# Opening of a mixer and expert-gather kernel reordered by tile, with half of a weight loaded a second time

## The reference

```python
p = (h @ w_in)                        # h: rmsnorm(x), scaled and shifted
rq, rk, rv, rg, gq, gk, gv, gg, lr_f, lr_b = split(p)
ret = head_rmsnorm(o_rf + flip(o_rb)) * silu(rg)     # retention, 4 heads x 128
gla = head_rmsnorm(o_gf + flip(o_gb)) * silu(gg)     # gated linear attention, 4 heads x 128
x = x + g1 * (concat([ret, gla]) @ w_out)
h = modulate(rmsnorm(x, norm2_w), sh2, sc2)
# peer_ffn, for each block of 128 tokens:
q = h @ w_q                                          # 8 heads x 2 halves x 128
s1, s2 = q[..., 0] @ k1.T, q[..., 1] @ k2.T          # 128 keys each
idx = top16 of (top16(s1) + top16(s2))               # one of 128 * 128 experts
act = gelu(einsum("thkd,td->thk", down[idx], h))
x = x + g2 * einsum("thkd->td", (softmax(top) * act) * up[idx])
```

## Time and profile before

| | |
|---|---|
| median of 3 runs | 3169.85 us (3169.84 to 3169.93) |
| span of the profiled execution | 3165.3 us |
| PE busy | 2588.5 us, 82% |
| DVE busy | 2022.9 us, 64% |
| ACT busy | 1229.5 us, 39% |
| POOL busy | 1074.3 us, 34% |
| software DMA queue (the gathers) | 1073.81 MB, 82.1% of 16 engines' span |

### The profile page before, as it was taken

The page is one execution under the profiler, slowest core; times in us unless marked ns, Lnnn a source line. Parts: engine busy times, 40 slices in busy tenths (PEclk is TensorE's granted clock), DMA queues, the critical chain, the costliest instruction groups (busy, mean ns, idle before and its releaser), DMA issues.

```text
span 3165.3 us, 35978 instructions
## 1 busy us (share of the span) xinstructions
PE 2588.5 (82%) x12092; PEld 1064.0 (34%) x12092; DVE 2022.9 (64%) x5008; ACT 1229.5 (39%) x3892; POOL 1074.3 (34%) x1041
## 2 busy tenths in 40 slices
PE   7999998878777877778988878888777877978777
PEld 3555653323222323223333344333223332322111
DVE  4533457777777777665555757667777776765544
ACT  3122335443443444334323533444344543443323
POOL 0000014433433444333433334343443443343331
PEclk9999999899999989999999999999999999999999
DMA  9411359999999999999999999999999999999995
GB/s 353 155 54 53 125 204 405 421 421 418 415 420 421 419 408 414 418 417 411 418 415 417 416 411 393 416 419 421 420 418 417 416 419 416 405 420 422 418 421 243
DMA packets 198780, 1179.94 MB, mean 373 GB/s; under 512 B 20994, under 2 KB 21700, under 8 KB 67268
## 3 DMA queue, kind: packets, MB, share of 16 engines
q0 software_dynamic: 147456, 1073.81, 82.1%
q1 hardware_dynamic: 51140, 103.84, 8.9%
HBM read 1175.48 MB, written 2.10 MB: 372 GB/s over the span
## 4 chain that ended last, share of the span: by engine, by line
DMA 47%; PE 14%; ACT 5%; DVE 4%; issue 3%; POOL 3%; DVEq 0%; POOLq 0%
DMA ring<-in_expert_rows,idx_v 18%; DMA ring<-in_peer_rows,idx_v 11%; DMA scr<-in_expert_rows,idx_v 9%; DMA scr<-in_peer_rows,idx_v 8%; PE banks L1166 8%; PE banks L814 6%; DVE ring L2299 2%; POOL ring L788 1%; DVE scr L2299 1%; DMA scr<-in_w_in 1%; POOL scr L788 1%; ACT ring L1688 1%; ACT L1682 1%; ACT scr L1682 1%; ACT L1644 1%
## 5 line engine op out<-in xcount | busy, mean ns | idle before, releaser
L1166 PE MATMUL banks<-ring 128*32 128x512 f32 x2016 | 809.5, 621 | 251.7 <-ACT ring L1688 241.4
L1166 PE MATMUL banks<-scr,ring 128*32 128x512 f32 x2080 | 819.8, 613 | 215.5 <-ACT ring L1688 214.8
L1682 ACT ACTIVATE scr<-scr 128x1 f32<-128x1 f32 x1024 | 206.9, 202 | 1511.9 <-DVE scr L2299 1510.4
L2299 DVE CUSTOM_DVE_ANT_0 scr<-scr,ring 128x1024 f32<-128x1024 f32 x390 | 478.0, 1226 | 305.9 <-DMA scr<-in_peer_rows,idx_v 157.4
L2299 DVE CUSTOM_DVE_ANT_0 ring<-ring 128x1024 f32<-128x1024 f32 x378 | 463.1, 1225 | 302.0 <-DMA ring<-in_expert_rows,idx_v 166.7
L788 POOL DMA_INDIRECT scr<-in_peer_rows,idx_v x264 | 272.7, 1033 | 475.9 <-PE banks L1166 355.7
L814 PE MATMUL banks<-hT,scr 128*128 128x128 f32 (+3 forms) x2576 | 367.7, 303 | 66.4 <-DVE ring L2281 47.3
L1166 PEld LDWEIGHTS banks<-ring 128*32 128x32 f32 x2016 | 162.8, 111 | 770.2 <-ACT ring L1688 486.8
L788 POOL DMA_INDIRECT ring<-in_expert_rows,idx_v x256 | 271.1, 1059 | 422.1 <-PE banks L1166 389.3
L1166 PEld LDWEIGHTS banks<-scr,ring 128*32 128x32 f32 x2080 | 165.9, 111 | 737.3 <-ACT ring L1688 458.4
L788 POOL DMA_INDIRECT ring<-in_peer_rows,idx_v x248 | 263.1, 1061 | 409.4 <-PE banks L1166 371.0
(11 more groups left out here) (255 smaller groups left out, 2247.4 us busy)
## 6 DMA issues: line engine op xcount, KB each, us to landing
scr<-in_w_in SPq DMA_DIRECT2D x8, 2048.0 KB, 28.4
scr<-in_w_mod SPq DMA_DIRECT2D x7, 2048.0 KB, 12.8
ring<-in_w_in SPq DMA_DIRECT2D x7, 2048.0 KB, 12.8
scr<-in_w_q SPq DMA_DIRECT2D x6, 2048.0 KB, 27.8
ring<-in_w_mod SPq DMA_DIRECT2D x5, 2048.0 KB, 13.2
scr<-in_peer_w_q SPq DMA_DIRECT2D x4, 2048.0 KB, 12.3
scr<-in_peer_rows,idx_v POOLq DMA_INDIRECT x264
ring<-in_w_out SPq DMA_DIRECT2D x2, 2048.0 KB, 7.8
```

Source lines behind the costliest of these rows:

```text
L1166: last = nc.tensor.matmul(psum[2 + c][32 * g:32 * g + 32, :], spread[:, i % 8, :], rows[slot_of(i)][:, D + c * CW:D + (c + 1) * CW], start ...
L1682: nc.scalar.activation(gelu[:, h, k:k + 1], dots[:, h, k:k + 1], ACT.Gelu if i < N_ROWS else ACT.Gelu_apprx_tanh).then_inc(gelu_done, 1)
L2299: V.tensor_tensor_reduce(u, u, xq[g], 1.0, 0.0, ALU.mult, ALU.add, dots[:, n % 2, k:k + 1]).then_inc(dotted, 1)
```

## The change

Seven edits belong together.

1. The gate gg is made between the steps of the GLA part, and rg after it; `gla_gate` takes the place of `ret_gate`.
2. After the GLA outputs only tile 0 is gated with rg (8 k-products), turned (8 transposes) and multiplied by w_out. The rg products of tiles 1 to 3 stand in pieces behind, between and after the scores of head 0 and its index (`ret_gate_part`), the turning of these tiles after the gate of head 0 is moved (`turn_heads`). The silu of rg is written in place in its PSUM bank.
3. w_out for tile 1 is made in the opening and by pair 9. The second halves of tiles 2 and 3 come at pairs 26 to 34, their first halves at pairs 70 to 76.
4. So the first half of w_out is loaded a second time (`w_out_again`), into slots 0 and 1, when the last row before row 80 in them is summed.
5. Rows 0 to 79 have the slots 4 to 7, 0 and 1; rows 80 to 175 the slots 4 to 7, 2 and 3; eight slots are in use from row 176. Before it was from row 38.
6. Additions, means, squares, roots and normed outputs of tiles 1 to 3 move to later pairs and rows with them.
7. The order of the chunk loads follows the new order of use.

```diff
 SLOTS = 8
-OPENING = 38
+HALF_LEFT = 80
+ALL_LEFT = 176
...
-          (("w_mod", CW * 11), 3), (("w_in", W_GQK), 0), (("w_in", W_RG), 2), (("w_in", W_GV), 1), (("w_out", 0), 0),
-          (("w_in", W_GG), 1), (("w_out", CW), 2)]
+          (("w_mod", CW * 11), 3), (("w_in", W_GQK), 0), (("w_out", CW), 2), (("w_in", W_GV), 1), (("w_in", W_GG), 0),
+          (("w_in", W_RG), 1), (("w_out", 0), 0), (("w_out_again", 0), 0)]
...
-    if i < 4:
+    if i < 2:
         return 4 + i
-    if i < OPENING:
-        return (4, 5, 6, 7, 0, 1)[(i - 4) % 6]
-    return (2, 3, 0, 1, 4, 5, 6, 7)[(i - OPENING) % SLOTS]
+    if i < HALF_LEFT:
+        return (6, 7, 4, 5, 0, 1)[(i - 2) % 6]
+    if i < ALL_LEFT:
+        return (6, 7, 4, 5, 2, 3)[(i - HALF_LEFT) % 6]
+    return (6, 7, 4, 5, 2, 3, 0, 1)[(i - ALL_LEFT) % SLOTS]
...
+            sp.wait_ge(summed, max(i for i in range(HALF_LEFT) if slot_of(i) < 2) + 1)
+            load_chunk("w_out_again", 0)
...
-                elif slot < 4:
-                    full(pool, "wo", TT - 1, slot // 2)
+                elif slot in (6, 7):
+                    full(pool, "yT", TT - 1, 1)
+                elif slot in (0, 1):
+                    full(pool, "wo", 1, 0)
+                elif slot in (2, 3):
+                    full(pool, "wo", TT - 1, 1)
+                if i >= ALL_LEFT and slot in (0, 1) and previous(i) < HALF_LEFT:
+                    full(pool, "wo", TT - 1, 0)
...
+            def turn_heads(t):
+
+                pe.wait_ge(y_done, 1 + t)
+                empty(pe, "rg", t)
+                for half, src in ((0, o_ret), (1, o_gla)):
+                    o = begin("yT", t, half)
+                    for h in range(HEADS):
+                        last = nc.tensor.transpose(o[:, h * P:(h + 1) * P], src[:, t, h * P:(h + 1) * P], ident)
+                    last.then_inc(bank_ready, 1)
+
+            ret_gate_part(0, 0, KT)
+            turn_heads(0)
...
                 project("wo", 0, w)
-                o = opened("wo", 1, 0)
-                for k in range(KT // 2):
-                    mm(o[:, :], yT[:, k, P:2 * P], w[0][:, k, :], k, KT)
+                ret_gate_part(1, 0, 4)
                 tile_rows("n1", 0)
+                ret_gate_part(1, 4, 6)
                 all_empty(pe, "nt", "n1", 0, 1)
                 scores_q(0)
                 scores_s(0)
-                project("wo", 2, w, (0,))
+                ret_gate_part(1, 6, KT)
+                ret_gate_part(2, 0, KT)
                 quad_rows(0, 0, 0)
+                quad_rows(0, 1, 2)
+                ret_gate_part(3, 0, 2)
                 move_idx(0)
-                quad_rows(0, 1, 2)
-                pe.wait_ge(idx_packed, 1)
+                ret_gate_part(3, 2, KT)
                 move_gate(0)
...
+                for t in (1, 2, 3):
+                    turn_heads(t)
                 pe.wait_ge(xq_set, 2)
                 quad_rows(0, 2, 2)
                 quad_rows(0, 3, 0)
+                empty(pe, "rg", 3)
                 scores_q(1)
                 scores_s(1)
-                add_batch(0)
-                project("wo", 3, w, (0,))
-                add_pair(2)
+                empty(pe, "yT", 1, 0)
+                empty(pe, "yT", 1, 1)
+                add_row(0, True)
+                add_row(1)
+                project("wo", 1, w, (0,))
+                add_pair(1)
                 move_idx(1)
                 move_gate(1)
                 scores_q(2)
                 scores_s(2)
-                add_pair(3)
-                project_part("wo", 1, w, 0)
+                add_batch(1)
                 add_batch(2)
                 scores_q(3)
                 add_pair(6)
-                project_part("wo", 1, w, 1)
+                project_part("wo", 1, w, 0)
                 add_pair(7)
...
+                      8: lambda: project_part("wo", 1, w, 1),
+                      70: lambda: first_half_again(0), 72: lambda: first_half_again(1),
+                      74: lambda: project_part("wo", 3, w, 0, 0), 76: lambda: project_part("wo", 3, w, 1, 0),
```

More of the change, by code:

```diff
@@ L340, in plan_jobs @@
             jobs.add(("go", c, odd), "A")
-    for t in range(TT):
-        jobs.add(("gg", t), "A")
-    for k in range(KT):
-        jobs.add(("yT", k), alternate(k))
+    jobs.add(("rg", 0), "D")
+    for half in range(2):
+        jobs.add(("yT", 0, half), "AD"[half])
     for n in range(2):
@@ L347, in plan_jobs @@
     tile("n1", 0, (0, 1))
+    for t, bank in ((1, 6), (2, 7), (3, 5)):
+        jobs.add(("rg", t), "D", bank)
+    for t in (1, 2, 3):
+        for half in range(2):
+            jobs.add(("yT", t, half), "AD"[half], 6 + half)
+    for n in range(2):
+        jobs.add(("wo", 1, n), "D", 6 + n)
+    tile("n1", 1, (6, 7), "AA")
     for t, n, bank in LAST_HALVES:
         jobs.add(("wo", t, n), "D", bank)
-    for t in (1, 2, 3):
+    for t in (2, 3):
         tile("n1", t, (6, 7), "AA")
@@ L636, in _ @@
         def _(sp):
-            wide = {"w_mod": a["w_mod"][0], "w_in": a["w_in"][0], "w_out": a["w_out"][0]}
+            wide = {"w_mod": a["w_mod"][0], "w_in": a["w_in"][0], "w_out": a["w_out"][0],
+                    "w_out_again": a["w_out"][0]}
             def load_chunk(name, c0):
                 n = chunk_number(name, c0)
-                if chunk_before(n) is not None:
+                if name == "w_out_again":
+                    full(sp, "wo", 1, 0)
+                elif chunk_before(n) is not None:
                     chunk_read(sp, chunk_before(n))
@@ L1081, in _, with ret_gate_part @@
                     from_scores(c, h, BWD).then_inc(bank_ready, 1)
-            w = use_chunk("w_in", W_GG)
-            to_rows([("gg", t) for t in range(TT)], hT, w, TT)
-            for k in range(KT):
-                o = begin("yT", k)
-                pe.wait_ge(y_done, 1 if k < HEADS else 1 + TT)
-                src = o_ret if k < HEADS else o_gla
-                for t in range(TT):
-                    last = nc.tensor.transpose(o[:, t * P:(t + 1) * P], src[:, t, (k % HEADS) * P:(k % HEADS + 1) * P], ident)
-                last.then_inc(bank_ready, 1)
+            w_rg = use_chunk("w_in", W_RG)
+            def ret_gate_part(t, first, last):
+                o = psum[jobs.bank[jobs.number("rg", t)]]
+                if first == 0:
+                    opened("rg", t)
+                if last == KT:
+                    begin("rg", t)
+                for k in range(first, last):
+                    ins = mm(o[:, :], hT[:, k, t * P:(t + 1) * P], w_rg[:, k, :], k, KT)
+                if last == KT:
+                    ins.then_inc(bank_ready, 1)
+            def turn_heads(t):
[8 more added lines that the diff above has]
+            turn_heads(0)
             def project(name, t, w, halves=(0, 1)):
@@ L1187, in next_quads @@
             def next_quads(it, g):
-                if g == 0:
+                if g == 0 and it == 1:
+                    empty(pe, "wo", 2, 1)
+                    empty(pe, "wo", 3, 1)
+                elif g == 0:
                     name, t = ("n1", 3) if it < TT else (("gf", 0) if it == TT else ("gf", 3))
@@ L1438, in _ @@
                       472: lambda: products(2), 489: lambda: products(TT - 1)}
-            for t, first in ((2, 8), (3, 13)):
+            for t, first in ((2, 26), (3, 32)):
                 beside[first] = lambda t=t: project_part("wo", t, w, 0)
@@ L1632, in _, with ret_silu, heads_out @@
             nc.scalar.activation(hstat[:, 2, TT * HEADS:], hstat[:, 1, TT * HEADS:], ACT.Sqrt).then_inc(head_root, 1)
[L1633 to L1640 removed]
+            def ret_silu(t):
+                o = full(act, "rg", t)
+                nc.scalar.activation(o[:, :], o[:, :], ACT.Silu).then_inc(rg_silu, 1)
+            def heads_out(t):
+                copy_out(yT[:, 0:HEADS, t * P:(t + 1) * P], "yT", t, 0).then_inc(emptied["A"], 1)
+            ret_silu(0)
+            heads_out(0)
             def softmax_exp(n):
@@ L2167, in _ @@
             head_roots(1)
-            for t in range(TT):
-                head_scale(TT + t)
-                dve.wait_ge(y_step, TT + t + 1)
-                empty(dve, "gg", t)
-                V.tensor_tensor(o_gla[:, t, :], o_gla[:, t, :], gate_tmp[:, t % 2, :], ALU.mult).then_inc(y_done, 1)
-            for k in range(1, KT, 2):
-                o = full(dve, "yT", k)
-                V.tensor_copy(yT[:, k, :], o[:, :]).then_inc(emptied["D"], 1)
+            dve.wait_ge(gla_gated, 1)
+            dve.wait_ge(y_step, TT)
+            gate_gla(0)
+            gate_ret(0)
+            heads_out(0)
+            for t in (1, 2, 3):
+                gate_gla(t)
             empty(dve, "g1", 1)
@@ L2527, in _ @@
                       959: lambda: tile_mean("fin", 2), 963: lambda: final(2)}
-            for t in (1, 2, 3):
-                beside[13 + 8 * t] = lambda t=t: tile_mean("n1", t)
-                beside[17 + 8 * t] = lambda t=t: tile_rstd("n1", t)
+            for t, first in ((1, 31), (2, 155), (3, 163)):
```

(2 more changed lines are left out.)

127 lines of the change are left out of this document (72 added, 55 removed).

## The result

| | before | after |
|---|---|---|
| median | 3169.85 us | 3187.08 us (3183.13 to 3188.51) |
| ratio | 1 | 1.0052, interval 1.0038 to 1.0066 |
| span of the profiled execution | 3165.3 us | 3181.4 us |

The account below looks back on a forecast made before the run. The prediction took the gather queue of 1,024 rows at 2.49 us each as the bound; lead -5.4, second load +5.0, six slots +2.5 and tile change +1.8 made +3.9, carried to 3173.8 us, range 3162 to 3185.

Parts of the forecast that it names:

- Start of the chain and the first gather: Opening: w_out for tile 0 starts at about 372.2, and the first gather is issued at 414.3, 16.3 us earlier.
- How much of the lead survives: Opening to row 10: of the 16.3 us head start, 5.4 us survive (-5.4), with row 10 issued at 459.1.
- rival C: Opening: tile 0 is early, but the lead is gone by row 24; +9.3 us, 3179.2, chance 0.08.
- The second load: From row 79 the queue has no hole, so loading half of w_out again, 2.1 MB, costs +5.0 us.
- Six slots: Rows 38 to 176: six slots give 417 GB/s against 420 with eight, +2.5 us; the tile change is costed separately.
- the +1.8 at the tile change: Row 128: slots come back late, so with six slots row 138 has its dot at 797.5, due 795.7; +1.8 us.
- the 14.94 us of six slots: Gather queue: with six slots a row must be issued, landed, dotted and summed in 6 x 2.49 us.
- the 1.2 us that I counted as in hand: Six-slot rows: a slot has 14.94 - 8.31 - 5.44 = 1.2 us spare, so moved work was costed at nothing.
- rival B: Six-slot rows: six slots starve the queue, issue to dot taking 7.20 us; +10.6 us, 3180.5, chance 0.20.
- its sign: Windows from 540 to 860 us under 415 GB/s would show that six slots starve the queue.
- The figure of 4.4 us: Gather of one 1.05 MB row: the skill's fit, 2.0 us plus bytes at 436 GB/s; tile change would cost 0.8.
- A's 3160.4: Opening: the queue never runs dry behind row 9, so the whole 16.3 us head start stays; 3160.4, chance 0.15.

Follow-up runs that it names:

- Experiment 4: The changed kernel with the second half of head 1's top-16 search put ahead of the addition of w_out's product for tile 1 on DVE: 1.0035, 11.1 us.
- experiments 1 and 3: 1: the changed kernel with the second load cut to 32 KB, 1.0037; 3: the kernel before with six slots until row 176 and the second load, 1.0046.
- experiments 9 and 10: 9: experiment 8's kernel with rows 0 and 1 summed before head 1's scores, 1.0010; 10: the same with the second load cut to 32 KB, 1.0001.
- experiment 2: The kernel before with one number changed, six slots until row 176 in place of row 38: 1.0032, 10.1 us.
- the second execution: Profiled execution of the changed kernel measured again without edit on another chip: 1.0053, 16.8 us above the kernel before.
- experiment 8: The changed kernel with head 1's index before the addition, second load after row 31, eight slots from row 56, first-half products at pairs 19 to 25: 1.0020.

## Why the prediction was wrong

- **Start of the chain and the first gather: right.** 370.0 and 412.4 against 372.2 and 414.3. In other executions of kernels with this opening up to the first gather it came at 415 to 418, so a few us of the opening belong to the execution, not to the order. Some steps of the working are 0.3 and 0.7 us more than their terms add up to (372.2 for 371.9, row 2 at 424.5 for 423.8), and the 1.7 us of score products is not in the earlier trace rows; none of it decides.
- **How much of the lead survives: the path was right, the size 4.3 us too large.** "So row 10 is issued at 459.1" failed by 3.1, 1.7 us because the index of head 1 reached PE at 452.7 and not at 451, and 1.8 because the query product behind PE's wait took 5.62 us and not the 3.81 of the row I took, less 0.4 that the working had put in too much (456.9 for 456.5). Another 1.1 us is row 10's 6.57 us to its dot where I took 5.44. Experiment 4 shows the cause on DVE: an addition that waits 6.46 us for PE stands ahead of the end of the search for that index. I had put it into the sum as 1.4 us of work and not as a wait. Row 24, which should have had its dot 5 to 7 us earlier, has it 1.6 us earlier in one execution and 1.6 later in the other. So the lead was as good as gone there, which is rival C's condition, at 0.08.
- **The second load: right at that place.** 5.1 and 4.4 us by the ratios (experiments 1 and 3), 4.4 to 6 us at its place in the traces, against 5.0. Part of it is won back later where slots are short (2.4 and 3.0 us by row 176, each in one pair of executions), which I had at nothing; and moved to row 32 it costs 2.8 us by the ratios (experiments 9 and 10).
- **Six slots: the step that failed.** "It is the nearest row in kind: 345 x 0.7% = +2.5" and the +1.8 at the tile change; together 4.3; experiment 2 measured 10.1 us. In its trace the first term measures 6.8 us before the tile change and 0.6 behind it, and the second 5.1. The window from 510 to 530 holds eight rows, and the rows that starve in experiment 2 lie 4 to 64 rows apart; it was too short to show them. The rows that could, 10 to 34 at 2.60 us each, I had set aside as the rest of the opening; carried over they give 15. Both terms that I set against the 14.94 us of six slots were too small. The 8.31 us from dot to issue are not the longest return before the tile change: row 64's is 10.77 in the same trace. And the "5.44 us from issue to dot" is that of a single row in an empty queue; where slots come back late in pairs the rows take 6.4 to 8.5. So the 1.2 us that I counted as in hand were not there. At the tile change I followed the slot of row 132; that of row 128 comes back after 11.08 us already in the kernel before, and in experiment 2 it starves row 134 as well. All this was rival B, to which I gave 0.20, and by its sign, 407 GB/s from 540 to 760, it came nearest. Its sum, 3180.5, lacks what the lead lost: 4.3 more is 3184.8.
- **The figure of 4.4 us.** It is the estimate from the fit in the Trainium skill ("DMA: Bandwidth & Descriptors", section "Anatomy of one DMA — SWDGE (gpsimd) path"). By it the tile change would have cost less still; the traces have 5.44 us from issue to dot in an empty queue and 6.4 to 8.5 for the late rows of this one, and they decide.
- **The rivals' sums.** A's 3160.4 leaves out the 2.5 us for the slots, which its condition does not touch; with them it is 3162.9. The others add up.
- **What stays open.** Lead, load and slots of the experiments make -1 + 4.7 + 10.1 = 13.8 of 16.8 us (4.7 is the mean of 5.1 and 4.4), and the ratios are known to 3 to 4 us on each side. The rest, some 3 us, may be the project parts and additions at rows 62 to 74 and 140 to 158. They were not tried alone, but the traces point at one of them: from row 158, behind which an addition of 1.4 us stands, to row 162 the changed kernel falls back by 2.8 and 3.2 us in its two executions, and experiment 2, which has no addition there, by nothing. By rows the loss does not split as in experiment 2 either: from row 34 to row 83 the changed kernel loses 3.1 us, experiment 2 6.1. That rows 96 to 176 lose less when the load has gone before them was seen in two pairs of traces and not explained. Why PE's granted clock fell in its wait is not settled either; only that it did (0.53 from 450 to 455 us, and 0.54 from 455 to 460 in the second execution, where the same wait of 4.5 us ends at 455.0), and that without the wait the product took 3.84 us.

## What to carry to other kernels

The queue of buffers here had a threshold, not a rate. Add the longest time from use to release, searched for over the whole stretch, and the time from issue to arrival of a row that is issued late, behind the two or three that are still in flight, not that of the empty queue; compare the sum with buffers times cadence (here 2.49 us a row). One buffer fewer cost nothing that could be told here, and the next one 10 us. And a head start is worth only what lies behind its first narrow place: follow the order on every engine until the queue is as full as before, and count an instruction that waits for another engine by its wait, with all that stands behind it. That holds for one's own repairs too (experiment 8).
